# Stick attention's squares summed on GpSimd, the recurrence's splits one turn up, the last rotation inside the local attention

## The reference, cut to what matters

```python
y_att = stick_breaking_attention(q, k, v).reshape(bsz, s, ATT_WIDTH)      # 8 heads of 64
y = jnp.concatenate([rms_norm(y_lru, norm_lru_out[l]),
                     rms_norm(y_att, norm_att_out[l])], axis=-1)
x = x + jnp.einsum('bse,ed->bsd', y, w_out[l])
...
h2 = rms_norm(x, norm_ffn[l])                                             # then a gated FFN
```

```python
y_na  = neighbourhood_attention(q_na, k_na, v_na, rpb)
q = apply_rope(rms_norm_2(q, q_gain), cos, sin)                           # grouped attention
k = apply_rope(rms_norm_2(k, k_gain), cos, sin)
y_mem = memory_attention(q_m, mk, mv)
```

## Time and profile before

| what | value |
|---|---|
| median of 3 runs | 1594.71 us (1593.8 to 1595.14) |
| profiled execution, time | 1594.15 us |
| profiled execution, span | 1592.3 us, 19870 instructions |
| TensorE busy | 1528.7 us, 96% |
| VectorE, ScalarE, GpSimd busy | 657.5, 498.4, 154.4 us |
| granted TensorE clock, mean | 0.994 of full |

### The profile page before, as it was taken

The page is one execution under the profiler, slowest core; times in us unless marked ns, Lnnn a source line. Parts: engine busy times, 40 slices in busy tenths (PEclk is TensorE's granted clock), DMA queues, the critical chain, the costliest instruction groups (busy, mean ns, idle before and its releaser), DMA issues.

```text
span 1592.3 us, 19870 instructions
## 1 busy us (share of the span) xinstructions
PE 1528.7 (96%) x7853; PEld 1069.5 (67%) x7853; DVE 657.5 (41%) x994; ACT 498.4 (31%) x807; POOL 154.4 (10%) x192
## 2 busy tenths in 40 slices
PE   7999999999999999989999999999999999899896
PEld 6788688888888888877777777887543343343333
DVE  6566855333334336574434454476102202201503
ACT  5634644222221215235444443334110010010112
POOL 3000000000000001143101221002000000021411
PEclk9999999999999999999999999999999999999998
DMA  7221233333333326233221112188799999999995
GB/s 216 95 91 54 80 93 92 94 106 90 96 106 97 88 80 198 80 106 106 80 67 54 41 54 80 40 293 328 304 414 396 417 421 421 421 421 420 421 421 198
DMA packets 137210, 305.87 MB, mean 192 GB/s; under 512 B 7488, under 2 KB 97488, under 8 KB 113568
## 3 DMA queue, kind: packets, MB, share of 16 engines
q1 hardware_dynamic: 133040, 294.99, 49.9%
q0 software_dynamic: 3504, 9.11, 2.1%
q10 hardware_dynamic: 576, 0.50, 0.1%
HBM read 298.28 MB, written 4.56 MB: 190 GB/s over the span
## 4 chain that ended last, share of the span: by engine, by line
PE 82%; DMA 8%; DVE 4%; ACT 3%; issue 2%; POOL 0%; SPq 0%; POOLq 0%; DVEq 0%; ACTq 0%
PE bank L2048 12%; PE bank L2050 12%; PE bank L2049 12%; PE bank L1263 12%; DMA RING<-w_down 6%; PE bank L2056 4%; PE bank L2058 4%; PE bank L2057 4%; PE bank L1284 4%; PE bank L2097 2%; PE bank L2198 2%; PE bank L2213 2%; PE bank L2067 2%; DMA RING<-w_gu 2%; PE bank L2069 2%
## 5 line engine op out<-in xcount | busy, mean ns | idle before, releaser
L2048 PE MATMUL bank<-XH,WH 128*128 128x512 f32 x768 | 303.5, 395 | 3.1 <-DVE XL L1870 2.0
L2050 PE MATMUL bank<-XH,WL 128*128 128x512 f32 x768 | 299.3, 390 | 0.0
L2049 PE MATMUL bank<-XL,WH 128*128 128x512 f32 x768 | 298.9, 389 | 0.0
L1691 DVE TENSOR_TENSOR WL<-RAW,WH 128x2048 fp32r<-128x2048 f32 (+1 forms) x90 | 191.6, 2129 | 134.5 <-ACT WH L1484 134.4
L1263 PE MATMUL bank<-RING,XS 128*64 128x512 f32 x496 | 222.5, 596 | 6.0 <-issue 4.4
L1264 PE MATMUL bank<-RING,XS 128*64 128x512 f32 x496 | 222.6, 597 | 0.0
L1484 ACT ACTIVATE WH<-RAW 128x2048 fp32r<-128x2048 f32 (+1 forms) x90 | 160.1, 1778 | 135.2 <-PE bank L2058 115.2
L2048 PEld LDWEIGHTS bank<-XH,WH 128*128 128x128 f32 x768 | 144.2, 188 | 35.8 <-issue 2.9
L2050 PEld LDWEIGHTS bank<-XH,WL 128*128 128x128 f32 x768 | 144.1, 188 | 30.5
L2049 PEld LDWEIGHTS bank<-XL,WH 128*128 128x128 f32 x768 | 144.3, 188 | 28.9 <-issue 0.2
L1263 PEld LDWEIGHTS bank<-RING,XS 128*64 128x64 f32 x496 | 64.2, 137 | 133.9 <-issue 131.5
(11 more groups left out here) (376 smaller groups left out, 2326.7 us busy)
## 6 DMA issues: line engine op xcount, KB each, us to landing
RING<-w_gu SPq DMA_DIRECT2D x124, 1024.0 KB, 19.2
RING<-w_down SPq DMA_DIRECT2D x60, 1024.0 KB, 22.7
RAW<-w_in SPq DMA_DIRECT2D x66, 512.0 KB, 4.7
RAW<-w_ffn_in SPq DMA_DIRECT2D x44, 512.0 KB, 4.7
RAW<-w_ffn_out SPq DMA_DIRECT2D x20, 512.0 KB, 4.3
RAW<-w_out SPq DMA_DIRECT2D x16, 512.0 KB, 4.7
RAW<-w_branch SPq DMA_DIRECT2D x24, 256.0 KB, 2.9
RAW<-w_memkv SPq DMA_DIRECT2D x8, 512.0 KB, 4.3
```

The lines of the kernel that those rows point to most:

```text
L1691: V.tensor_tensor(WL[:, u % 2, :n], RAW[:, u % 2, :n], WH[:, u % 2, :n].bitcast(F32), ALU.subtract).then_inc(s["w_lo"], 1)
L2048: T.matmul(bank[:, :st.nt], wh[:, k, c], hi, start=k == 0, stop=False)
L2049: T.matmul(bank[:, :st.nt], wh[:, k, c], lo, start=False, stop=False)
L2050: ins = T.matmul(bank[:, :st.nt], wl[:, k, c], hi, start=False, stop=k == st.K - 1)
```

## The change

It has three parts.

1. The squares of stick attention's first four turns (head pair 0) are written to a new tile `SQT`, one place for each query tile. Those of the other twelve go to one of two `SQ` buffers, and GpSimd adds them to the place of their query tile. The ones product leaves the turns; `asum` has four, behind a wait for the twelfth addition. VectorE copies four columns where it reduced sixteen. ScalarE waits, from turn 6 on, until the buffer that it will overwrite has been added.
2. The step `lsplit` moves from fill 8 to fill 7.
3. `rope_tile(3)` moves from behind the first `na_band()` to the end of the local attention's fill 0, behind the first half of `nav(1)`.

```diff
-    SQ = at("SQ", 80, [P, P])
+    SQ = at("SQ", 185.5, [P, 2, P])
+    SQT = at("SQT", 186.5, [P, TT, P])
...
-            8: [norm_sum, lambda: add("lsplit", dict(yhi=4, ylo=4), after=qkv[1]), memk(1)],
+            7: [lambda: add("lsplit", dict(yhi=4, ylo=4), after=qkv[1])],
+            8: [norm_sum, memk(1)],
...
     whole(nav(0))
-    na_band()
-    rope_tile(3)
-    na_band()
-    na_band()
-    na_band()
+    for _ in range(4):
+        na_band()
     small = pieces_of(nav(1), nak(1), naq(1), *(gate(0, j) for j in range(4)), gate(1, 0), gate(1, 1))
     fill = {i: [f] for i, f in enumerate(small)}
+    fill[0].append(lambda: rope_tile(3))
...
+            elif st.kind == "O" and st.a.att == "stick" and st.a.n >= TT:
+                pool.wait_ge(s["sq"], st.a.n + 1)
+                sums = SQT[:, st.a.qt[0], :]
+                nc.gpsimd.tensor_tensor(sums, sums, SQ[:, st.a.n % 2, :], ALU.add).then_inc(s["sqt"], 1)
...
-                A(SQ[:, :], src, ACT.Square).then_inc(s["sq"], 1)
+                n = st.a.n
+                if n >= TT + 2:
+                    act.wait_ge(s["sqt"], n - TT - 1)
+                A(SQ[:, n % 2, :] if n >= TT else SQT[:, st.a.qt[0], :], src, ACT.Square).then_inc(s["sq"], 1)
...
-                V.tensor_reduce(ST[:, 124:128], PV[:, 256:272].rearrange("p (h t) -> p t h", h=4), AX,
-                                ALU.add).then_inc(s["asq"], 1)
+                V.tensor_copy(ST[:, 124:128], PV[:, 256:260]).then_inc(s["asq"], 1)
...
-                square_sum(atts[15]).then_inc(s["ass"], 1)
+                pe.wait_ge(s["sqt"], 3 * TT)
+                for t in range(TT):
+                    ins = T.matmul(PV[:, 256 + t:257 + t], SQT[:, t, :], ones[:, 0:1], start=True, stop=True)
+                ins.then_inc(s["ass"], 1)
...
-                if a.att == "stick" and a.n:
-                    ins = square_sum(atts[a.n - 1])
```

More of the change, by code:

```diff
@@ L226, in build @@
                ms_hi ms_lo saved band0 band1 x2h x2l lgp lgs afp af top ixp rtok cols colg rcp pn ohi t1A t1D wrp xt_ps xtA xtD lgc lg2 sq ass rat lrs asq arc fms fsd fnr ftn fnrm""".split()
-    names.extend(["rms_q", "rsd_q"])
+    names.extend(["rms_q", "rsd_q", "sqt"])
     s = {n: sem(n) for n in names}
@@ L2097, in scores @@
             T.matmul(o, q, kk, start=True, stop=True).then_inc(s["qk"], 1)
[L2099 to L2103, removed]
         def values(a, j, kt):
```

## The result

The median of the changed kernel is 1598.79 us (20 runs, 1597.01 to 1601.75), against 1595.18 us (20 runs, 1593.8 to 1597.06) of the kernel before. The ratio is 1.0021, with a 95% interval from 1.0015 to 1.0027. So the change makes the kernel 0.0021 x 1595.18 = 3.4 us slower (2.4 to 4.3 by the interval), where I forecast 1.2 us. The measured 0.21% lies just on the bound between "within 0.2%" and "slower by over 0.2%", and the interval reaches to both sides of it. The profiled execution took 1598.04 us (span 1596.2, mean granted clock 0.992), against 1594.15, 1592.3 and 0.994.

A forecast was written before the change was run, and what follows sets the result against it. TensorE, busy 96% of the span, was taken to bound the kernel. Parts of -1.45, 0 and +2.6 (0.9 chain plus 1.7 clock) summed to +1.15 on 1594.71, so 1595.9 us; outer range 1592.8 to 1598.7.

The forecast's parts named there:

- the mechanism's own range: Whole kernel: 1594.0 to 1597.8 us around the summed forecast, which was given chance 0.54.
- gross 2.4 us: Stick attention: ten ones products of 0.24 us each won on TensorE, before 0.65 is given back at the end.
- An addition then costs VectorE 0.1: Stick attention: each GpSimd addition slows VectorE by 0.1 us, 0.3 us in all on the path.
- the 0.90: A pair of 128x256 VectorE additions took 0.90 us while GpSimd scaled probabilities, against 0.74 with GpSimd only issuing transfers.
- 5 of 15 as swallowed: Stick attention: five of the 15 removed ones products win nothing, as TensorE then waits for something else; ten win 0.24 each.
- The row that the forecast held against this page: VectorE's pair of 128x256 additions beside GpSimd: 0.16 us slower on 0.74, agreeing in sign with the page's contention warning.
- both orders meeting at the next transposes: Stick attention, after turn 9's scores: old and new order of the splits coincide where VectorE decides, so part 2 costs 0.
- it starts 2.3 to 2.5 us late: Stick attention, turn 8: the mem-key product waits for delayed sigmoids and starts at about 166.5 instead of 164.19.
- upper bound of +0.9: Part 2's worst case: 2.5 us late minus the 1.6 us wait, with nothing caught up.
- The chain: Start of local attention: VectorE's sequence with the moved rotation brings the first transposes at 710.56 against 709.67, 0.9 us late.
- the clock's term: Local attention: 3.5 us at half speed behind TensorE's stop of about 6 us lose 1.7 us; bounds 0 and 3.4.
- slower rival: Local attention: table load inside VectorE's rotation (+1.28) and slow clock twice as long (+1.7), total +4.1, 1598.8 us; chance 0.14.

The follow-up runs named there:

- after: The whole change against the kernel before, as traced in its profiled execution of 1598.04 us; ratio 1.0021.
- squares_no_adds: Part 1 alone on the kernel before, without GpSimd's twelve additions and the waits on them; ratio 0.9990.
- p1_warm: Part 1 alone on the kernel before, with seven idle products on TensorE ahead of turn 9's output product; ratio 0.9997.
- p2_warm: Part 2 alone on the kernel before, with eight idle products on TensorE ahead of the second mem-key product; ratio 1.0001.
- p3_warm: Part 3 alone on the kernel before, with 20 idle products on TensorE between turn 2's two local scores; ratio 1.0011.
- all_warm: The whole change with eight idle products ahead of the mem-key product and 20 between turn 2's local scores, against the kernel before; ratio 0.9994.
- p1_squares: Only part 1 applied to the kernel before; ratio 0.9999.
- p1_rot_fill3: Part 1 on the kernel before, with the rotation in the local attention's fill 3 behind the second half of the key product; ratio 0.9989.
- p1_rot_before_keys: Part 1 on the kernel before, with the rotation first in the local attention's fill 3, ahead of the second key half; ratio 0.9959.
- p3_rotation: Only part 3 applied to the kernel before; ratio 1.0019.
- rot_before_keys: Only the rotation moved in the kernel before, to the head of the local attention's fill 3, ahead of the second key half; ratio 0.9967.
- p2_splits: Only part 2 applied to the kernel before; ratio 1.0019.

## Why the prediction was right, and where it was wrong

In two of three parts the mechanism was as forecast and a size was off; in part 2 a step was missing. On the forecast's scale the measured ratio gives 1594.71 x 1.0021 = 1598.1 us. That is outside the mechanism's own range (1594.0 to 1597.8) and inside the outer one (to 1598.7). All errors went the same way, so that the outer range held is in part luck.

**Part 1, -1.45 forecast, -1.0 in the stretch at full clock.** The mechanism was right: 8 records in place of 32, and a net gain on TensorE under the gross 2.4 us. Two terms were too good. "An addition then costs VectorE 0.1" came from a row that I misread. The second of the two instructions behind the 0.90 of the earlier trace rows started only when TensorE's scores were over (707.49 + 1.40 = 708.89 in the earlier trace rows), so the 0.90 holds a wait, and each of the two took its usual time. The row of L1791 in the kernel before, 708.4 to 709.2 us (busy us, then mean ns of one, then idle before):

```profile
L1791 DVE TENSOR_TENSOR PB<-bank,B 128x256 f32<-128x256 f32 x2 | 0.8, 414 | 0.1
```

What an addition really costs VectorE, where it costs anything, is 0.22 to 0.27. The timelines of POOL and DVE in after:

```profile
176.12 1.00 POOL L1429 TENSOR_TENSOR SQT<-SQT,SQ 128x128 f32<-128x128 f32 x1 [9.93 <-ACT SQ L1663]
```

```profile
165.80 1.48 DVE L1772 TENSOR_TENSOR_SCAN SC<-SK,MSK 128x512 f32<-128x512 f32 x1
...
176.78 1.23 DVE L1778 TENSOR_TENSOR PB<-SE,SC 128x384 f32<-128x384 f32 x2
```

The same scan of the other head in that turn took 1.22. The pair of products took 1.00 in the kernel before:

```profile
163.29 1.22 DVE L1765 TENSOR_TENSOR_SCAN SC<-SK,MSK 128x512 f32<-128x512 f32 x1
...
176.68 1.00 DVE L1771 TENSOR_TENSOR PB<-SE,SC 128x384 f32<-128x384 f32 x2
```

In after, six of the twelve additions lengthen one VectorE instruction each in this way. All six of these read two tiles in SBUF; an instruction that reads a bank, as `YAL<-bank,VEC,YAH` does, kept its 0.34 to 0.35 us beside an addition. Eight additions take 0.45 to 0.50 us, as forecast from the earlier trace rows, and four take 0.65 to 1.00. On the path all twelve cost 0.42 (squares_no_adds). And "5 of 15 as swallowed": without any addition the stretch wins 1.27 where my count gives 1.75, so about two more products of 0.24 are swallowed, or their place is taken by the clock in turn 9. p1_warm shows which when the clock is full. From scores to scores, turn 11 takes 2.52 us and turn 14 takes 5.67, against 2.36 and 5.63 in the kernel before, so nothing is won there; turn 11 has the wait of 0.67 for VectorE. The Trainium skill, "GPSIMD Engine Reference", Key points, warns that GpSimd contends with VectorE instructions of two SBUF inputs; the 0.26 on a scan and the 0.23 on the products agree with it. The row that the forecast held against this page reads a bank and is not the page's case.

**Part 2, 0 forecast; +2.53 alone, +1.30 in the whole.** Every step in the text happened: sigmoids late, mem-key product behind a wait of 2.36 us, weight wait of turn 9 gone, both orders meeting at the next transposes (p2_warm). The step that failed is what is missing behind "it starts 2.3 to 2.5 us late": TensorE stands still in that time. I put a slow clock behind the 2.46 us stop of part 3 from the earlier trace rows, and did not put one behind the new stop of the same length. The upper bound of +0.9 was too low for that reason.

**Part 3, +2.6 forecast, +3.24 in the whole, +3.48 alone.** The chain was right to its steps: first maxima at 690.54 (690.4 in the text), VN evacuated at 698.80 (698.65), the second half of nav(1) over at 702.99 (703), a stop of 5.53 (about 6), transposes at 710.69, or 710.55 on the old scale, where stretch B starts 0.14 later (710.56). p3_warm has the 0.9 by itself. Only the clock's term was short: 8.40 - 6.04 = 2.36 us in place of 1.7. The half clock lasted from ahead of 706.5 into the stretch from 713.5 and so hit more of the products than the 3.5 us that I took from the earlier trace rows.

That a chain of VectorE hid the slow clock before, as the forecast says, shows in p1_warm. PE behind the stop of turn 1:

```profile
698.20:705.00 6.80, 5.85 (x24) 0.50 0.49 116
```

The half clock lasted twice as long as in the earlier trace rows, behind a stop of the same 2.47 us, and B is 149.37 us as ever.

The table loads cost nothing that the stretch shows (the chain of p3_warm is +0.88 with them, the forecast's 0.9 without). The timeline of ACT in after:

```profile
696.58 1.28 ACT L1640 ACT_TABLE_LOAD   x1
701.51 0.30 ACT L1640 ACTIVATE ST<-ST,CST 128x10 f32<-128x10 f32 x1 [3.65 <-DVE ST L1840]
```

The Sqrt load ran ahead of the wait of its root, as at 213.62 in the earlier trace rows. So of the slower rival's two mechanisms one (a longer slow clock) came, the other (the load inside the rotation) did not; its 1598.8 us was near for a reason that is half another one, the clock in part 2.

**The sum.** By all_warm and after, in the stretches: squares and splits at full clock -1.14, chain of the rotation +0.89, clock behind the rotation +2.35, clock behind the mem-key stop +1.30, together +3.40, as measured there. What separates the result from my +1.15 is thus mainly 1.3 + 0.65 of clock and 0.3 in the rest of stretch A. With both clock terms taken away, -0.25 remains, where the forecast without its 1.7 was -0.55.

**Not settled.** The ratios of the parts alone add up to -0.2 + 3.0 + 3.0 = 5.8 us and the whole has 3.4. In the profiles 1.1 of this lies in part 2: the product behind its stop took 8.49 us alone and 7.39 in the whole, behind stops of 2.14 and 2.36, with the clock at half for 6.7 and 3.4 us. Why it lasts longer in one than in the other I did not find, and the intervals of three ratios (0.0009 each, 1.4 us) could hold most of the rest.

## What to carry to other kernels

Before moving work so that one wait replaces another, ask how long TensorE will stand in one piece and what follows it: here a stop of 2 us or more could cost another 1.3 to 2.6 us in the products behind it, which no chain of waits shows, and it is hidden only if another engine's chain decides there anyway. Put a long block of another engine beside the longest product that TensorE must do in any case, and ahead of it in the queue (the same rotation was worth +3.5 us in one fill, +0.2 in another, -5.2 in a third). A few idle products in the stop separate the clock from the wait in one experiment.

## What the runs showed of the hardware

- The fall of the clock is not the same in every execution. Behind turn 9's wait of 2.0 us it fell in p1_squares, p1_rot_fill3 and squares_no_adds, not in p1_rot_before_keys; behind the wait of 1.6 us it fell in p3_warm, not in the kernel before, p3_rotation and rot_before_keys, whose instructions up to there are the same. It fell to 0.50 each time. On the products behind it that cost 1.46 (after, mem-key) to 2.56 us (p2_splits), where nothing hid it.
- How long it stays at half is not the same either. Behind the mem-key stop it was 3.4 us in after and 6.7 in p2_splits. Behind the stop of 2.46 or 2.47 us in the local attention's turn 1 it was 3.5 us before and 6.8 in p1_warm.
- Products whose result nobody reads kept the granted clock at 1.00 behind the stops that they filled, in p1_warm, p2_warm, p3_warm and all_warm.
- A 128x128 addition took GpSimd 0.45 to 0.50 us in eight of twelve places of after, and 0.65 to 1.00 in four, each begun beside a VectorE instruction that reads two SBUF tiles. Six of the twelve lengthened one such instruction by 0.22 to 0.27 us.
